# Four down projections of a two-layer block: six of eleven row pairs by seven products in place of eight

## The chip, the cores and the metric

The kernel runs on one core of one Trainium2 chip. Its time is the device time of one execution in microseconds (us); lower is better. The engines are TensorE (PE; its weight loads are listed as PEld), VectorE (DVE), ScalarE (ACT), GpSimd (POOL) and SyncE (SP, which here issues nearly all DMAs).

## The reference, cut to what matters

The program is two layers of a block (feed-forward, mixer, feed-forward, gated embedding), followed by a third block with three attention branches and an MLP, on 256 tokens of width 1024. The change touches the four feed-forwards alone. Each is

```python
def swiglu(x, w_gu, w_down):
    g, u = jnp.split(x @ w_gu, 2, axis=-1)
    return (jax.nn.silu(g) * u) @ w_down

h = h + 0.5 * swiglu(rmsnorm(h, ffn1_norm[i]), ffn1_w_gu[i], ffn1_w_down[i])
```

with `w_gu` of 1024 x 5632 and `w_down` of 2816 x 1024. The product with `w_down` is the down projection: 256 tokens (two blocks of 128) by 22 chunks of 128 rows of `w_down` by 1024 columns (two halves of 512). All of it is float32.

## The kernel before, in words

**A float32 product as three.** TensorE multiplies in a format of fewer bits (`F32R`), so each operand is split into a high part, the value rounded, and a low part, the rest. A product is high x high + high x low + low x high: three matmuls, all added up in one bank of PSUM. The activation (stationary, 128 x 128) and the weights (moving, 128 x 512) are split alike.

**The stream of weight tiles.** `plan_of` lists every weight tile of the program in the order of use, up to 128 x 2048 numbers (1 MB) each. For tile n, SP loads it into one of four slots of `raw` (`load`), ACT copies it to one of three slots of `whi` (high part, ACT's `ahead`, recorded at L1412), DVE subtracts to one of three slots of `wlo` (low part, DVE's `ahead`, L1967), and PE multiplies with both (L564). `take(label)` in an engine's program means: bring this engine's share up to two tiles beyond that label, and for PE wait for that tile. A copy of tile n waits until PE has released tile n - 3. Each engine works strictly through its own list.

**A feed-forward** (`ffn` in each engine's program). For each of 11 chunks c of 256 columns, PE does the up product (two tiles, 48 matmuls), ACT applies Silu (`ftmp`), DVE multiplies by the other half (`fa`), PE transposes `fa` with four transposes (L567, `turn_a`) into bank 4 or 5, and ACT and DVE split the result into `aThi` and `aTlo` (`high_a`, `low_a`). Then comes the down projection (`down`): for column half 0, six weight tiles, token blocks 0 and 1 into banks 6 and 7; then for half 1 six tiles into banks 2 and 3. The last two tiles of a half are taken together, token block 0 first (`closing_block`). In all 44 pairs of chunk and half, 2 token blocks, 3 matmuls: 264 matmuls of 512 columns. Each half is added to the residual `h` by DVE (`residual`, L1970). The transposes of `h` for the next norm (`turn(r, t, 0)`) and what is computed from them (`early_quarters`: `hThi`, `hTlo`) lie in the second half's tiles.

**Where.** The plan is `plan_of` at L156, PE's program `tensor` with `down` at L724 and `ffn` at L743, ACT's `down` at L1466 and `ffn` at L1488, DVE's `down` at L2021 and `ffn` at L2051, POOL's at L2558. The relative-bias table of the attention layer is loaded by SP in `table` (L517), during the up products of the third feed-forward. A small `rstds` on POOL computes the norms' roots.

Of the kernel before, what the change touches and what calls it, by code (L numbers as in the profile page):

```python
# [18 lines left out]
TILE = 2048  # L19

# [23 lines left out]
def constants():  # L44
# [30 lines left out]
    "a_weigh": "exps", "v_outputs": "yev yg yTlo", "a_outputs": "yThi ysq",  # L75
# [69 lines left out]
class Plan:  # L145


    def __init__(self):
        self.tiles, self.index = [], {}

    def add(self, label, pieces, a, b):
        self.index[label] = len(self.tiles)
        self.tiles.append((pieces, a, b))


def plan_of(dr):  # L156
    p = Plan()

    def ffn(i, up, down, extra=None):
        for c in range(11):  # L160
            if extra is not None and c in (0, 2):
                p.add(("pproj", extra, c // 2), [wsrc(dr["ple_w_proj"][extra], 0, 2, c * 256, 512)], 2, 512)
            for k in range(2):
                p.add(("up", i, c, k), [wsrc(up, 4 * k, 4, x * 2816 + c * 256, 256) for x in range(2)], 4, 512)
        for c in range(2):
            for y in range(6):
                nk = min(4, 22 - 4 * y)
                p.add(("down", i, c, y), [wsrc(down, 4 * y, nk, c * 512, 512)], nk, 512)
# [55 lines left out]
PREP = (8, 16, 24)  # L224
HALVES = 2 * len(PREP) + 2
# [129 lines left out]
def programs(dr, mem, banks, plan, ev):  # L355
# [11 lines left out]
    pool_tiles = set()  # L367

    def wview(name, n):
        _, a, b = plan.tiles[n]  # L370
        slots = NRAW if name == "raw" else NSPL
        return mem[name][:, n % slots, 0:a * b].rearrange("p (a b) -> p a b", a=a)

    def wflat(name, n, slots):
        _, a, b = plan.tiles[n]
        return mem[name][:, n % slots, 0:a * b]
# [117 lines left out]
    def sync(S):  # L494
# [3 lines left out]
        def load(n):  # L498
            pieces, a, b = plan.tiles[n]
            slot = wflat("raw", n, NRAW).rearrange("p (a b) -> p a b", a=a)  # L500
            if n >= NRAW:
                last = (n - NRAW,) if n - NRAW > 1 else (n - NRAW, 3)
                S.wait_ge(*at("w_hi", *last))
                S.wait_ge(*at("w_lo" if n - NRAW not in pool_tiles else "w_lo_p", *last))
            c = 0
            for src in pieces:
                wd = src.shape[2]
                e.dma_start(slot[:, :, c:c + wd], src).then_inc(*sig(f"d_w{n % NRAW}", n, by=16))
                c += wd
# [7 lines left out]
        def table():  # L517
            rp = dr["rpb"]
            S.wait_ge(*at("h", 4, 1, 1))
            for y in range(2):  # L520
                src = bass.AP(rp.tensor, 464 - 249 - 15 - (4 - y) * 31, [[1, 64], [465, 16], [1, 250]])
                e.dma_start(mem["tb"][64 * y:64 * y + 64, :, 0:250], src).then_inc(*sig("d_tb", y, by=16))
# [20 lines left out]
        for n in range(2, len(plan.tiles)):  # L543
            if n == tile["yout", 7] + 5:
                pos(0)
            if n == tile["up", 2, 0, 0] + 8:
                table()
            if n == tile["down", 2, 0, 0]:
                pos(1)
            load(n)  # L550
# [9 lines left out]
    def tensor(T):  # L560
# [13 lines left out]
        def take(*label):  # L574
            n = T.n
            T.n += 1
            if tile[label] != n:
                raise ValueError(label)
            T.wait_ge(*at("w_hi", n))
            T.wait_ge(*at("w_lo_p" if n in pool_tiles else "w_lo", n))  # L580
            return wview("whi", n), wview("wlo", n)
# [114 lines left out]
        def closing_block(labels, bs, xhi, xlo, first, between=None):  # L696

            held, k0 = [], first
            for label in labels:
                hi, lo = take(*label)  # L700
                held.append((label, hi, lo, k0))
                k0 += hi.shape[1]
            for t in range(2):
                for i, (label, hi, lo, kk) in enumerate(held):
                    nk = hi.shape[1]
                    for k in range(nk):
                        xh, xl = (y[:, kk + k, t * P:(t + 1) * P] for y in (xhi, xlo))
                        mm(banks[bs[t]], xh, hi[:, k, :], kk + k == 0, False)
                        mm(banks[bs[t]], xh, lo[:, k, :], False, False)
                        last = mm(banks[bs[t]], xl, hi[:, k, :], False, kk + k + 1 == k0)  # L710
                        if between and t and i == 0 and k == 1:
                            between()
                    if t:
                        last.then_inc(*sig(*named(label)))
                    elif i == len(held) - 1:
                        last.then_inc(*sig(*half(label, 0)))
# [7 lines left out]
        def down(name, xhi, xlo, tiles, r, turn_last):  # L724

            for c in range(2):
                bs = ACC[c]
                clear(*bs)
                for y in range(tiles - 2):
# [3 lines left out]
                    if y == 0:  # L733
                        if c == 0:
                            turn_last()
                        elif r < 10:
                            turn(r, 0, 0)
                            turn(r, 1, 0)
                closing_block([name + (c, tiles - 2), name + (c, tiles - 1)], bs, xhi, xlo, 4 * (tiles - 2),
                              (lambda: turn(1, 0, 1)) if c and r == 1 else None)  # L740
                residual_in(r, c, bs)

        def ffn(i, r, extra=None):  # L743
# [24 lines left out]
            down(("down", i), aThi, aTlo, 6, r + 1, lambda: turn_a(10))  # L768
# [636 lines left out]
    def scalar(A):  # L1405
# [8 lines left out]
        def ahead(m):  # L1414
            while A.ready < min(m, len(plan.tiles)):
                n = A.ready
                A.ready += 1
                A.wait_ge(*at(f"d_w{n % NRAW}", n))
                if n >= NSPL:
                    A.wait_ge(*at(*named(plan_labels[n - NSPL])))  # L1420
                copy(wflat("whi", n, NSPL), wflat("raw", n, NRAW)).then_inc(*sig("w_hi", n))
# [44 lines left out]
        def down(name, tiles, r):  # L1466
            for c in range(2):
                for y in range(tiles):
                    if r == 1 and c and y == tiles - 1:
                        square(1, 0, 1)  # L1470
                        high(1, 0, 1)
                    take(*name, c, y)
                    if c and y == 1:
                        if r != 10:
                            early_quarters(r)
                        early_squares(r)
                    if c == 0 and y == 0:
                        yield
            if r == 10:
                square(r, 0, 1)  # L1480
                square(r, 1, 1)
            elif r == 1:
                square(1, 1, 1)
                high(1, 1, 1)
            else:
                late_quarters(r)

        def ffn(i, r, extra=None):  # L1488
            fa, aThi = mem["fa"], mem["aThi"]

            def high_a(c):
                A.wait_ge(*at("turn_a", i, c))
                copy(flat(aThi[:, 2 * c:2 * c + 2, :]), banks[4 + c % 2]).then_inc(*sig("aThi", i, c))
# [17 lines left out]
            for _ in down(("down", i), 6, r + 1):  # L1511
                high_a(10)
# [406 lines left out]
        plan_labels = list(plan.index)  # L1919
# [43 lines left out]
    def vector(V):  # L1963
# [7 lines left out]

        def ahead(m):
            while V.ready < min(m, len(plan.tiles)):
                n = V.ready
                V.ready += 1
                if n in pool_tiles:
                    continue
                V.wait_ge(*at("w_hi", n))
                tt(wflat("wlo", n, NSPL), wflat("raw", n, NRAW), f(wflat("whi", n, NSPL)), ALU.subtract).then_inc(*sig("w_lo", n))
# [41 lines left out]
        def down(name, tiles, r, scalars):  # L2021

            for c in range(2):
                for y in range(tiles):
# [7 lines left out]
                    if c and y == 1 and r != 10:  # L2032
                        early_quarters(r)
            for t in range(2):
                residual(r, t, 1, half(name + (1, tiles - 1), t), ACC[1][t], scalars[t])
                if r == 10:
                    mean_square(10, t)
                if r == 1 and t == 0:
                    low(1, 0, 1)
                    mean_square(1, 0)  # L2040
            if r == 1:
                scaled(0)
            take(*name, 1, tiles - 1)
            if r == 1:
                mean_square(1, 1)
                low(1, 1, 1)
                scaled(1)
            elif r != 10:
                late_quarters(r)

        def ffn(i, r, extra=None):  # L2051
            fa, aThi, aTlo = mem["fa"], mem["aThi"], mem["aTlo"]

            def low_a(c):
                V.wait_ge(*at("aThi", i, c))
                tt(flat(aTlo[:, 2 * c:2 * c + 2, :]), banks[4 + c % 2], f(flat(aThi[:, 2 * c:2 * c + 2, :])), ALU.subtract).then_inc(*sig("aTlo", i, c))
# [16 lines left out]
            for _ in down(("down", i), 6, r + 1, (0.5, 0.5)):  # L2073
                low_a(10)
# [485 lines left out]
    def gpsimd(G):  # L2560
# [5 lines left out]
        def ahead(m):  # L2566
            while G.ready < min(m, len(plan.tiles)):
                n = G.ready
                G.ready += 1
                if n in pool_tiles:  # L2570
                    G.wait_ge(*at("w_hi", n))
                    tt(wflat("wlo", n, NSPL), wflat("raw", n, NRAW), f(wflat("whi", n, NSPL)), ALU.subtract).then_inc(*sig("w_lo_p", n))

        def take(*label):
            ahead(tile[label] + NSPL)

# [59 lines left out]
        def three():  # L2636
            for what, n in three_steps():
                if what == "gate" and n % 2 == 0:
                    take("gate", n // 2)
                elif what == "keep" and n in (3, 7):  # L2640
# [4 lines left out]

        rstds(0)
        rstds(1)
        ssd()
        rstds(2)
        ple_rstd(0)  # L2650
        for r in (3, 4, 5):
            rstds(r)
        natt()
        rstds(6)
        ple_rstd(1)
# [9 lines left out]
def layout(nc):  # L2665
# [29 lines left out]
    def phase(*items):  # L2695
# [3 lines left out]
        if o > 229368:  # L2699
# [4 lines left out]
          ("sg", [P, 2, D]), ("xn", [P, 2, D]), ("pT", [P, 2, 256]), ("pThi", [P, 2, 256], F32R), ("pTlo", [P, 2, 256], F32R))  # L2704
    put("rThi", [P, 8, 256], F32R, z + 48 * 1024)
# [107 lines left out]
```

## Time and profile before

| what | value |
|---|---|
| median of 3 runs | 1677.99 us (1677.39 to 1678.73) |
| profiled execution, first to last instruction (span) | 1676.1 us |
| median less span (what lies around it) | 1.9 us |
| PE busy | 1664.8 us, 99% |
| DVE busy | 1068.0 us, 64% |
| ACT busy | 898.6 us, 54% |
| POOL busy | 86.1 us, 5% |
| mean granted TensorE clock | 0.998 |

The profiled execution's own device time is not listed separately; its span is, and the median of the runs stands 1.9 us above it. Busy time is the time in which an engine had an instruction at work; matmuls overlap in the pipeline, so a busy PE says that it was never out of work, and not how fast it went. Where rows say "idle before <- X", the engine waited that long and X ended the wait. In the rows of the timeline, an instruction that follows its predecessor without a wait starts about 0.08 us before the predecessor's listed end.

### The profile page before, as it was taken

The page shows a single profiled execution, that of the slowest core. Times are in us where ns is not written, and L with a number is a line of the kernel's source. Part 1 is how long each engine was busy: PE and PEld are TensorE (multiplying, and loading weights), DVE is VectorE, ACT ScalarE, POOL GpSimd, SP SyncE. Part 2 cuts the span into 40 slices and gives each one's busy share as a digit, 9 for nine tenths or more (in the row PEclk, how much of TensorE's full clock was granted, in tenths as well). Part 3 has the DMA queues.
Part 4 walks back from the last instruction along what each step waited for, and adds up shares of the span by engine and source line. Part 5 has one row for each costly group of instructions (what it writes and reads, how often), then busy time and mean ns, then how long its engine had stood idle before and what let it go on. Part 6 is the DMA issues. An engine that isn't in the chain of part 4 may idle for free.

```text
span 1676.1 us, 23021 instructions
## 1 busy us (share of the span) xinstructions
PE 1664.8 (99%) x9366; PEld 1426.7 (85%) x9366; DVE 1068.0 (64%) x1364; ACT 898.6 (54%) x1279; POOL 86.1 (5%) x79
## 2 busy tenths in 40 slices
PE   8999999999999999999999999999999999999998
PEld 6888899999788888888888778888889999988886
DVE  5554678999965545755457766555655577766643
ACT  5443566777864444744346665444553556564532
POOL 0000000000100000000007500000000000000000
PEclk9999999999999999999999999999999999999999
DMA  9655567666466554686555336655565533465551
GB/s 306 192 178 184 158 191 208 179 196 209 156 200 198 187 188 165 188 242 209 181 175 195 119 101 214 185 180 188 180 197 153 174 103 126 152 211 178 176 192 60
DMA packets 243978, 300.58 MB, mean 179 GB/s; under 512 B 9248, under 2 KB 175520, under 8 KB 243872
## 3 DMA queue, kind: packets, MB, share of 16 engines
q1 hardware_dynamic: 238224, 289.25, 54.5%
q10 hardware_dynamic: 5648, 9.85, 2.2%
q8 instruction: 75, 1.23, 0.3%
q14 instruction: 31, 0.25, 0.0%
HBM read 297.96 MB, written 1.11 MB: 178 GB/s over the span
## 4 chain that ended last, share of the span: by engine, by line
PE 99%; DVE 1%; DMA 0%; ACT 0%; ACTq 0%; DVEq 0%; issue 0%
PE bank L564 95%; PE bank L567 4%; DMA h<-in_x 0%; DVE wlo L1967 0%; DVE hTlo L1970 0%; DVE xn L1970 0%; DVE h L1970 0%; ACT hThi L1412 0%; DVE xn L2019 0%; DVEq L2740 0%; ACT xn L1409 0%; ACTq L1924 0%; ACTq L1923 0%; ACT L1920 0%; ACTq L2740 0%
## 5 line engine op out<-in xcount | busy, mean ns | idle before, releaser
L1967 DVE TENSOR_TENSOR wlo<-raw,whi 128x2048 fp32r<-128x2048 f32 (+2 forms) x284 | 622.4, 2195 | 326.5 <-ACT whi L1412 326.5
L1412 ACT ACTIVATE whi<-raw 128x2048 fp32r<-128x2048 f32 (+2 forms) x284 | 518.2, 1832 | 244.8 <-PE bank L564 240.9
L564 PE MATMUL bank<-whi,hThi 128*128 128x512 f32 x1056 | 420.7, 398 | 0.0
L564 PE MATMUL bank<-wlo,hThi 128*128 128x512 f32 x1056 | 412.3, 390 | 0.3 <-DVE wlo L1967 0.3
L564 PE MATMUL bank<-whi,hTlo 128*128 128x512 f32 x1056 | 396.8, 391 | 0.0
L564 PE MATMUL bank<-hThi,whi 128*128 128x256 f32 x888 | 253.3, 285 | 0.0
L564 PE MATMUL bank<-hThi,wlo 128*128 128x256 f32 x888 | 251.2, 283 | 0.0
L564 PE MATMUL bank<-hTlo,whi 128*128 128x256 f32 x888 | 251.2, 283 | 0.0
L564 PEld LDWEIGHTS bank<-whi,hThi 128*128 128x128 f32 x1056 | 198.6, 188 | 44.3 <-issue 6.0
L564 PEld LDWEIGHTS bank<-whi,hTlo 128*128 128x128 f32 x1056 | 198.5, 188 | 42.6 <-DVE hTlo L1970 0.3
L564 PEld LDWEIGHTS bank<-wlo,hThi 128*128 128x128 f32 x1056 | 198.8, 188 | 40.5 <-DVE wlo L1967 1.8
L564 PEld LDWEIGHTS bank<-hThi,whi 128*128 128x128 f32 x888 | 169.5, 191 | 3.6 <-issue 3.1
L564 PEld LDWEIGHTS bank<-hThi,wlo 128*128 128x128 f32 x888 | 169.5, 191 | 0.2
L564 PEld LDWEIGHTS bank<-hTlo,whi 128*128 128x128 f32 x888 | 169.5, 191 | 0.2
L564 PE MATMUL bank<-whi,aThi 128*128 128x512 f32 x352 | 137.8, 391 | 0.0
L564 PE MATMUL bank<-whi,aTlo 128*128 128x512 f32 x352 | 137.1, 389 | 0.0
L564 PE MATMUL bank<-wlo,aThi 128*128 128x512 f32 x352 | 137.0, 389 | 0.0
L1412 ACT ACTIVATE aThi<-bank 128x512 fp32r<-128x512 f32 x44 | 26.3, 598 | 155.1 <-PE bank L567 155.1
L1409 ACT ACTIVATE ftmp<-bank,st 128x256 f32<-128x256 f32 x88 | 41.5, 475 | 105.6 <-PE bank L564 105.5
L2564 POOL TENSOR_TENSOR st<-st,cst 128x1 f32<-128x1 f32 (+2 forms) x35 | 36.5, 1057 | 1147.4 <-DVE st L1992 1075.2
L1967 DVE TENSOR_TENSOR aTlo<-bank,aThi 128x512 fp32r<-128x512 f32 x44 | 30.4, 691 | 80.8 <-ACT aThi L1412 80.8
L564 PEld LDWEIGHTS bank<-whi,aTlo 128*128 128x128 f32 x352 | 66.1, 188 | 13.8
(222 smaller groups left out, 1883.4 us busy)
## 6 DMA issues: line engine op xcount, KB each, us to landing
raw<-in_ffn_w_gu SPq DMA_DIRECT2D x172, 512.0 KB, 4.9
raw<-in_ffn_w_down SPq DMA_DIRECT2D x40, 1024.0 KB, 5.0
raw<-in_w_in SPq DMA_DIRECT2D x30, 1024.0 KB, 5.2
raw<-in_ssd_w_in SPq DMA_DIRECT2D x16, 1024.0 KB, 5.6
raw<-in_ssd_w_in SPq DMA_DIRECT2D x32, 512.0 KB, 5.5
raw<-in_w_up SPq DMA_DIRECT2D x16, 1024.0 KB, 5.4
raw<-in_w_down SPq DMA_DIRECT2D x16, 1024.0 KB, 5.0
raw<-in_na_w_qkv SPq DMA_DIRECT2D x12, 1024.0 KB, 5.2
```

The source lines that it names most:

```text
L564: return T.e.matmul(out, lhsT, rhs, start=start, stop=stop, skip_group_check=skip)
L567: return T.e.transpose(out, in_, ident)
L1409: return e.activation(out, in_, func, **kw)
L1412: return e.activation(out, in_, ACT.Identity, **kw)
L1967: return e.tensor_tensor(out, a, b, op)
L2564: return e.tensor_tensor(out, a, b, op)
```

## The change

For six pairs of chunks (2j, 2j + 1), j = 0 to 5, the 2 x 2 x 2 block product (two token blocks, two chunks, two column halves) is computed with seven block products in place of eight, by the scheme of Winograd: a block product is three matmuls as before. The scheme needs four combinations of the weight blocks and four combinations of the activation blocks, and its result in four PSUM banks more (0, 1, 4, 5) that are combined at the end.

- **Plan.** The 1 MB tile `paired` of pair j holds all four weight blocks. It is followed by a tile `mixed` that has no load: its 128 x 2048 numbers are the four combinations, computed by DVE (`sums`) from `raw` into a buffer `ts0` to `ts2`: one instruction of 1024 columns and two of 512, each waiting for the one before. Of `paired` only 1536 columns are split, of `mixed` all 2048. PE uses `paired` for three block products (9 matmuls) and `mixed` for four (12).
- **Order.** The other ten chunks (12 to 21) stay classic, in six tiles of 2 or 4 chunks: `down 0 0`, pair 0, `down 1 0`, pairs 1 and 2, `down 0 1`, pairs 3 to 5, `down 0 2`, and at the end `down 1 1` with `down 1 2`. The transposes of `h` now lie in the last of these.
- **Activations.** During the up products of chunks 1 to 6, ACT copies the transposed bank to `araw`, POOL computes the combinations (`differences`: three subtractions), and ACT and DVE split them (`high_d`, `low_d`).
- **Merging.** After the last pair, ACT copies bank 0 at half scale, DVE does six operations of 512 columns (`merged`), and POOL two additions. Then the residual of the classic products follows.
- **Elsewhere.** The bias table's load moves from the third feed-forward's up products to the start of the attention layer; the row and the transposed embedding of `pos(1)` are loaded there too. An unused branch for tiles split on POOL goes.

```diff
+        rest(0, 0)
+        for j in range(PAIRS):
+            p.add(("paired", i, j), [wsrc(down, 2 * j, 2, 512, 512), wsrc(down, 2 * j, 2, 0, 512)], 2, 1024)
+            p.add(("mixed", i, j), None, 4, 512)
+            if j == 0:
+                rest(1, 0)
+            if j == 2:
+                rest(0, 1)
+        rest(0, 2)
+        rest(1, 1)
+        rest(1, 2)
...
+REST = {(0, 0): (12, 4), (0, 1): (16, 2), (0, 2): (18, 4), (1, 0): (12, 4), (1, 1): (16, 4), (1, 2): (20, 2)}
...
@@ sync: load, table
+                if labels[m][0] == "paired":
+                    S.wait_ge(*at("tsum", *labels[m][1:]))
...
-            S.wait_ge(*at("h", 4, 1, 1))
+            S.wait_ge(*at("w_rel", "mixed", 2, PAIRS - 1))
...
-            if n == tile["up", 2, 0, 0] + 8:
+            if n == tile["qkv", NA_CHUNKS[1], 0]:
                 table()
-            if n == tile["down", 2, 0, 0]:
                 pos(1)
...
@@ tensor: mixed_down
+            def seven(j):
+                first, final = j == 0, j == PAIRS - 1
+                hi, lo = take("paired", i, j)
+                T.wait_ge(*at("aTlo", i, j))
+                T.wait_ge(*at("dTlo", i, j))
+                three_products(0, block_of(2 * j, 0), hi[:, 0, 512:1024], lo[:, 0, 512:1024], first, final)
+                three_products(2, difference(j, 2), hi[:, 1, 0:512], lo[:, 1, 0:512], first, False)
+                three_products(6, block_of(2 * j + 1, 0), hi[:, 1, 512:1024], lo[:, 1, 512:1024], False, False).then_inc(
+                    *sig("w_rel", "paired", i, j))
+                hi, lo = take("mixed", i, j)
+                if first:
+                    clear(4)
+                three_products(4, difference(j, 0), hi[:, 0, :], lo[:, 0, :], first, final)
+                three_products(5, block_of(2 * j, 1), hi[:, 1, :], lo[:, 1, :], first, final)
+                three_products(1, difference(j, 1), hi[:, 2, :], lo[:, 2, :], first, final)
+                three_products(7, block_of(2 * j + 1, 1), hi[:, 3, :], lo[:, 3, :], False, False).then_inc(*sig("w_rel", "mixed", i, j))
...
+            for t in range(2):
+                for k, (hi, lo, y) in enumerate(held):
+                    last = three_products(2 + t, block_of(k0 + k, t), hi, lo, False, k == len(held) - 1)
+                    if t == 0 and k == 2:
+                        turn(r, 0, 0)
+                    if t == 0 and k == 3:
+                        turn(r, 1, 0)
...
@@ scalar: ahead waits for landed(n); for a mixed tile that is "tsum"
+                copy(mem["araw"][:, c % 2, :], b).then_inc(*sig("araw", i, c))
+                copy(aThi[:, 2 * c, 0:P], b[:, 0:P])
+                copy(aThi[:, 2 * c + 1, :], b[:, 256:512]).then_inc(*sig("aThi", i, c))
...
+            def high_d(c):
+                A.wait_ge(*at("dsum", i, c))
+                d = mem["dsum"][:, c % 2, :]
+                copy(aThi[:, 2 * c, P:256], d[:, 0:P])
+                copy(flat(mem["dThi"][:, c, :, :]), d[:, P:512]).then_inc(*sig("dThi", i, c))
...
@@ vector
+        def sums(n):
+            i, j = labels[n][1:]
+            w, o = mem["raw"][:, plan.raw_of[n] % NRAW, :], mem[f"ts{j % 3}"][:, :]
...
+            tt(halves(o[:, 0:1024]), halves(w[:, 512:1536]), w[:, 0:512].unsqueeze(1).to_broadcast([P, 2, 512]), ALU.add).then_inc(*sig("tfirst", i, j))
+            V.wait_ge(*at("tfirst", i, j))
+            tt(o[:, 1024:1536], o[:, 0:512], w[:, 1024:1536], ALU.add).then_inc(*sig("tsecond", i, j))
+            V.wait_ge(*at("tsecond", i, j))
+            tt(o[:, 1536:2048], o[:, 1024:1536], w[:, 1536:2048], ALU.add).then_inc(*sig("tsum", i, j))
...
         def ahead(m):
             while V.ready < min(m, len(plan.tiles)):
                 n = V.ready
                 V.ready += 1
-                if n in pool_tiles:
-                    continue
+                if labels[n][0] == "paired":
+                    sums(n)
                 V.wait_ge(*at("w_hi", n))
...
+            def merged():
+                um, wm = flat(mem["ftmp"][:, :, :]), flat(fa[:, :, :])
+                V.wait_ge(*at("root", i))
+                stt(h[:, 0, chunk(0)], banks[0], 0.5, h[:, 0, chunk(0)], ALU.mult, ALU.add).then_inc(*sig("h11", i))
+                V.wait_ge(*at("w_rel", "mixed", i, PAIRS - 1))
+                stt(um, banks[1], 0.5, um, ALU.mult, ALU.subtract).then_inc(*sig("um", i))
+                stt(h[:, 0, chunk(1)], banks[4], 0.5, h[:, 0, chunk(1)], ALU.mult, ALU.add).then_inc(*sig("h12p", i))
...
+            def mixed_down(r):
+                take("down", i, 0, 0)
+                low_a(10)
+                for j in range(PAIRS):
+                    take("paired", i, j)
+                    take("mixed", i, j)
...
+                merged()
+                take("down", i, 0, 2)
+                V.wait_ge(*at("h21", i))
+                for t in range(2):
+                    residual(r, t, 0, half(("down", i, 0, 2), t), 6 + t, 0.5)
...
@@ gpsimd
+            tt(pairs(d[:, 0:256]), a[:, P:256].unsqueeze(1).to_broadcast([P, 2, P]), outer, ALU.subtract).then_inc(*sig("dpair", i, c))
+            G.wait_ge(*at("dpair", i, c))
+            tt(d[:, 256:384], a[:, 384:512], d[:, 0:P], ALU.subtract).then_inc(*sig("droot", i, c))
+            G.wait_ge(*at("droot", i, c))
+            tt(d[:, 384:512], a[:, 256:384], d[:, 256:384], ALU.subtract).then_inc(*sig("dsum", i, c))
```

## Rows read from the trace of the kernel before

**Rows 1.** The page: its span and the engines' busy time.

```profile
span 1676.1 us, 23021 instructions
PE 1664.8 (99%) x9366; PEld 1426.7 (85%) x9366; DVE 1068.0 (64%) x1364; ACT 898.6 (54%) x1279; POOL 86.1 (5%) x79
```

**Rows 2.** The page: the chain that ended last, by engine.

```profile
PE 99%; DVE 1%; DMA 0%; ACT 0%; ACTq 0%; DVEq 0%; issue 0%
```

**Rows 3.** Chain in order of time, 128 to 215 us: start, length, what.

```profile
131.61 10.93 PE bank L564 x48
142.98 29.96 PE bank L564 x132
173.81 21.78 PE bank L564 x96
195.59 0.44 PE bank L567 x4
196.03 2.77 PE bank L564 x12
```

**Rows 4.** Timeline of ACT, 128 to 210 us: start, length, what, idle before.

```profile
143.01 0.60 ACT L1412 ACTIVATE aThi<-bank 128x512 fp32r<-128x512 f32 x1 [3.60 <-PE bank L567]
143.51 1.91 ACT L1412 ACTIVATE whi<-raw 128x2048 fp32r<-128x2048 f32 x1
```

**Rows 5.** The same of DVE.

```profile
143.65 0.69 DVE L1967 TENSOR_TENSOR aTlo<-bank,aThi 128x512 fp32r<-128x512 f32 x1 [1.90 <-ACT aThi L1412]
145.45 2.29 DVE L1967 TENSOR_TENSOR wlo<-raw,whi 128x2048 fp32r<-128x2048 f32 x1 [1.11 <-ACT whi L1412]
155.08 1.23 DVE L1967 TENSOR_TENSOR wlo<-raw,whi 128x1024 fp32r<-128x1024 f32 x1 [2.29 <-ACT whi L1412]
168.18 2.29 DVE L1967 TENSOR_TENSOR wlo<-raw,whi 128x2048 fp32r<-128x2048 f32 x1 [4.51 <-ACT whi L1412]
170.39 1.28 DVE L1970 SCALAR_TENSOR_TENSOR h<-bank,h 128x512 f32<-128x512 f32 x2
199.43 0.88 DVE L2019 TENSOR_SCALAR xn<-h,st 128x512 f32<-128x512 f32 x2
```

**Rows 6.** Timeline of DVE, 600 to 690 us: an add that waits for DVE itself.

```profile
679.75 0.74 DVE L1970 SCALAR_TENSOR_TENSOR sg<-sg,st,pp 128x512 f32<-128x512 f32 x1
680.53 0.69 DVE L1967 TENSOR_TENSOR h<-h,sg 128x512 f32<-128x512 f32 x1
```

**Rows 7.** Chain in order of time, whole run: the second and the last down projection.

```profile
610.64 29.96 PE bank L564 x132
1133.40 29.97 PE bank L564 x132
```

**Rows 8.** Groups by form: busy us, mean ns, idle before.

```profile
L2564 POOL TENSOR_TENSOR gate<-gate 128x512 f32<-128x512 f32 x6 | 9.7, 1616 | 248.8 <-DVE EW L1967 244.9 <-ACT gate L1409 4.0
```

**Rows 9.** Stretches: busy us (count) of PE, PEld, DVE, ACT, POOL, PEclk, DMA, GB/s.

```profile
20.00:130.00 110.00, 110.00 (x503) 90.82 (x502) 62.84 (x52) 53.88 (x58) 1.06 (x2) 1.00 0.66 211
4.00:8.00 4.00, 1.48 (x7) 0.67 (x5) 0.00 (x0) 0.78 (x4) 0.00 (x0) 1.00 0.97 316
8.00:10.00 2.00, 1.76 (x6) 1.21 (x6) 1.61 (x5) 1.48 (x6) 0.00 (x0) 0.51 1.06 373
```

**Rows 10.** Timeline of the opening, two matmuls of 512 columns.

```profile
10.76 0.63 PE L564 MATMUL bank<-whi,hThi 128*128 128x512 f32 x1
11.19 0.51 PE L564 MATMUL bank<-whi,hTlo 128*128 128x512 f32 x1
```

**Rows 11.** Timelines of POOL and of DVE from 895 us: both at work.

```profile
895.95 7.29 POOL L2564 TENSOR_TENSOR bm<-tb,cst 128x256 f32<-128x256 f32 x8
...
896.68 2.75 DVE L1967 TENSOR_TENSOR wlo<-raw,whi 128x2048 fp32r<-128x2048 f32 x1
```

**Rows 12.** DMA issues: count, KB each, us to landing.

```profile
raw<-in_ffn_w_down SPq DMA_DIRECT2D x40, 1024.0 KB, 5.0
tb<-in_rpb SPq DMA_DIRECT2D x2, 1000.0 KB, 14.6
```


## What was predicted

> **What bounds the kernel now.** I read the page's busy times first. The reader is to see PE at work for 1664.8 of 1676.1 us while DVE has 64% [rows 1]; then the chain that ended last, which gives PE 99% [rows 2]. So a matmul less is worth its spacing, as long as no other engine takes the end of that stage. The chain in order of time shows the first down projection as unbroken blocks of matmuls [rows 3]: 132 in 29.96 us, 0.227 us each. The second and the last look the same, 29.96 and 29.97 us [rows 7], so one walk serves all four. Last I read DVE and ACT in that stretch [rows 4, 5]: they sleep between tiles and wait for PE to release a slot. That slack is what the change spends.
>
> **What is removed.** A pair goes from 24 matmuls to 21, so a projection loses 18 and the program 72. At 0.227 us that is 4.09 us per projection, 16.3 us in all, if nothing is late.
>
> **What is added on DVE.** Prices: 128x2048 takes 2.29 us alone and 2.21 us to the next one's start; 1024 columns 1.23 [rows 5]; 512 columns 0.69, between plain float32 tiles in SBUF too, with a start 0.04 us after the end of what it waits for on its own engine (679.75 + 0.74 to 680.53) [rows 6]. By these slopes 1536 columns are 1.76. ACT takes 1.91 for 2048 and starts its next some 0.1 before the end [rows 4]; DVE starts 0.02 to 0.04 after ACT's end. One pair on DVE:
> - sums: 1.23 + 0.04 + 0.69 + 0.04 + 0.69 = 2.69 us;
> - the low part of `paired` starts 0.08 before that end and takes 1.76: over at 4.37;
> - meanwhile ACT can copy `mixed` only from 2.69 + 0.03, for 1.92: done at 4.64;
> - the low part of `mixed` starts at 4.68 and gives DVE free 2.21 later: 6.89 us.
>
> PE needs 21 x 0.227 = 4.77 us for the pair. Before, the same 1 MB of weights cost DVE 2.21 against 5.45 on PE. So inside the pairs DVE is the bound by 2.1 us a pair. The classic tiles between give back 5.45 - 2.21 = 3.2 (one of 4 chunks), 2.72 - 1.14 = 1.6 (one of 2).
>
> **The walk through one projection**, on the clock of the first. Up to the transposes of chunk 10 nothing changes for PE: sums of pair 0 and its low part run from 132.9 to 137.3 in the stretch where DVE waited before; the last `fa` is out near 138.1, and PE transposes it only at 142.5. `aTlo` of chunk 10 comes at 143.65, and the next low part (now `down 1 0`) at 145.45, as before [rows 5]. From there DVE has no idle time but what is inside a pair:
> - `down 1 0`: 145.45 + 2.21 = 147.66;
> - pairs 1 to 5: 5 x 6.89 = 34.45, and `down 0 1`: 1.14. Together 183.25;
> - `down 0 2` and `down 1 1`: 4.42. 187.67;
> - `merged`, six of 512 columns, 0.61 apart as the two residuals of 1.28 show [rows 5], with a wait or two inside: 3.66. 191.33;
> - `down 1 2`: 1.22, and 0.04 to PE: 192.59.
>
> PE on the same clock: pair 0 from 142.95, `down 1 0` 147.77 to 153.21, pair 1 to 157.98. It would start pair 2 there but gets its low part at 158.9: the first stall. From then it waits some 0.6 us before each `mixed` and, after `down 0 1`, 1.6 before each of pairs 4 and 5. `down 0 2` runs from 186.1 to 191.5, and then PE waits to 192.59, because it takes `down 1 1` and `down 1 2` at once. 36 matmuls (8.17) and two groups of transposes (0.88) follow: 201.64. Before, the same point, without the third group of transposes (0.44), was 196.03 + 2.77 - 0.44 = 198.36 [rows 3]. So a projection becomes 3.28 us **longer**: 4.1 won in matmuls, 7.4 lost in stalls.
>
> What is queued behind DVE's waits: in a pair, the `mixed` low part waits for ACT's copy with the next pair's sums behind it, for which PE waits. In `merged` DVE waits for ACT's copy of bank 0 (from 184.7) and the last matmul of pair 5 (186.1), both past at 187.7, so these cost nothing. POOL's two additions (1.62 each [rows 8]) end near 193, before DVE asks for them at 198.4.
>
> **Transposes and next stage.** `h` of half 0 is ready at 193.2 and 193.8, PE turns it at 194.6 and 195.8, and the split is over at 198.5; the next stage begins after 201.6. Cost nothing; if DVE came 3 us later still, PE would also wait at the turn. In the first projection alone the transposes of `h` 0, half 1 come six matmuls into block 1, at 198.9, and its residual, held behind that split, is out at 199.1: 0.2 us more.
>
> **The up products.** DVE has 62.84 busy of 110 us there, ACT 53.88, POOL 1.06 [rows 9]; a chunk is 11.37 us (10.93 + 0.44), so ACT works 5.6 of it. It gains four copies of at most 512 columns (under 0.60 each [rows 4]), DVE 0.8 us or so, POOL three subtractions of under 1.62 [rows 8]. From the transposes (131.6) by 0.60 + 3 x 1.62 the combination is there at 137.1, and ACT asks for it after `ftmp` at 137.6. Its weight copies come up to 0.8 us later, with PE over 5 us behind. Cost nothing; should POOL be twice as slow, ACT's next copy would come 4 us later and still in time.
>
> **DMA.** Bytes are the same; 1 MB in 6.9 us is slower than before, and a load lands 5.0 us after issue [rows 12] while four slots give over 10 us. The table (2 loads, 14.6 us to landing [rows 12]), `pos(1)` and two weight tiles now go out together near the third projection's end. POOL took the table at 895.95 [rows 11], about 16 us into the attention stage; it would land before. I cost it at 0, its bounds being 0 and 5 us (a tile that comes one landing late).
>
> **Sum.** 4 x 3.28 + 0.2 = 13.3 us. The span goes from 1676.1 to 1689.4; the median stood 1.9 above the span, so 1678.0 + 13.3 = 1691.3 us.
>
> **Unknown prices, both ends.** The trace shows no sum of float32 tiles with a repeated operand. From below: one-source operations on SBUF took 0.44 us per 512 columns (the last of [rows 5]); at that rate the three sums save 1.02 us a pair, 5 x 1.02 = 5.1 a projection, -1.8 in place of +3.3: 1671. From above: with POOL at work 2048 columns took 2.75 for 2.29 [rows 11], a factor 1.20; on the sums +0.52 a pair, 2.6 a projection: 1702. I take 0.69, because the addition `h<-h,sg` is the same kind of instruction on the same memory [rows 6], and POOL is idle during the pairs. The Trainium skill, "VectorE: DVE Perf Modes", section "Mode 2×_2P — use both read ports for one tensor", says that float32 operations of one source can go at twice the rate while a two-source one can't, its second port being busy. These rows agree (0.44 against 0.69), which speaks against the lower end.
>
> **The rivals.**
> - Only the matmuls count. DVE hides all of it: -16.3 us, 1661.7. For it: DVE idles half of the stretch now. Against: 6.89 against 4.77 in a pair, and at most three tiles of `wlo` to run ahead on. 3%.
> - The other side: cheap sums. The mechanism sits in `sums`; it decides from 3.28 / 5 = 0.66 us less per pair, so below 6.23 us the kernel is faster, down to 1671. 4%. Around that point, within 0.2%, lie 4%.
> - Dear sums or dear waits: a pair of 7.4 us, 1698 to 1702. 9%.
> - The clock. In the opening PE worked 1.48 of 4 us, and then the granted clock was 0.51, the level of 1.2 GHz, with 0.43 us between matmuls [rows 9, 10]. If the gaps (PE at work 69% of a pair) did this from pair 1 to `down 0 2`, 141 matmuls would take 60.6 us where the walk has 39.4: 21 us more a projection, 1776. Against: every other stretch was at 1.00, and no gap here passes 1.6 us. 4%. The Trainium skill's "TensorE: Matmul & The Clock Gate", section "A second HAM failure mode: psum-queue depth-cycling", describes frequent small idle times that make the clock swing; no row of this trace shows it in mid-kernel.
>
> **How the numbers follow.** DVE as the bound, at the prices read: 76%, 1685 to 1698 (a pair of 6.6 to 7.2 us, and the table). The range for 8 in 10 reaches up into dear sums: 1684 to 1702. About 0.2%, 3.4 us, is what a measurement can tell from no change. Slower: 76 + 9 + 4, 89%; same 4%; faster 3 + 4, 7%.
>
> **What would show it.** 72 matmuls of 512 columns fewer; PE at 97 to 98% busy with idle time released by DVE `wlo`, some 7 us in each projection and none elsewhere; DVE in a pair 6.9 us from sum to sum with ACT's copy of `mixed` on its path; the chain running through DVE between pair 2 and `down 1 2`. Wrong it is if the sums of 512 columns last well under 0.69, if PE shows no gaps, if the clock falls, or if gaps appear in the up products or at the start of the attention stage.

## The result

| kernel | median, us | fastest to slowest | ratio to before, 95% interval |
|---|---|---|---|
| before | 1678.36 | 1677.39 to 1679.18 | |
| changed | 1700.28 | 1698.92 to 1701.60 | 1.013 [1.0116, 1.0144] |

The change makes the kernel slower by 21.9 us; forecast were 13.3, with a range of 1684 to 1702. The page of the changed kernel, its span, the engines' busy time and the chain by engine (against [rows 1, 2]):

```profile
span 1696.7 us, 23401 instructions
PE 1659.9 (98%) x9294; PEld 1411.4 (83%) x9294; DVE 1203.5 (71%) x1556; ACT 959.6 (57%) x1403; POOL 138.6 (8%) x159
...
PE 86%; DVE 8%; ACT 3%; issue 2%; DMA 0%; ACTq 0%; DVEq 0%
```

72 matmuls went. The span grew all the same, and 14% of the chain runs through other engines, where it was 1%.

**Where the time went.** From PE's timeline I took, for each of the four projections, the time from its first matmul's start to 0.227 us after its last one's start, and the stretches between. All in us:

| | projection 1 | 2 | 3 | 4 | between 1, 2 | between 2, 3 | between 3, 4 | after 4, to the last matmul's start |
|---|---|---|---|---|---|---|---|---|
| before | 61.69 | 61.21 | 61.25 | 61.26 | 405.97 | 149.59 | 250.71 | 480.13 |
| changed | 66.91 | 67.52 | 65.93 | 65.93 | 405.96 | 149.63 | 250.70 | 480.15 |

Everything outside the projections is the same within 0.04 us. The projections cost 5.22, 6.31, 4.68 and 4.67 more, 20.9 together, and the spans differ by 20.6 (the opening took 0.3 less). The medians differ by 21.9: the profiled execution of the changed kernel, 1698.92 us, is the fastest of its four, and where the others take their 0.5 to 2.7 us more no trace shows. Three parts are to be told apart: 4.67 in each, 0.54 more in the first, 1.6 more in the second.

DVE in the first projection (start, length, what, idle before; it answers to [rows 5]):

```profile
145.12 2.29 DVE L2109 TENSOR_TENSOR wlo<-raw,whi 128x2048 fp32r<-128x2048 f32 x1 [1.11 <-ACT whi L1524]
147.33 1.22 DVE L2109 TENSOR_TENSOR ts<-raw 128x1024 f32<-128x1024 f32 x1
148.59 1.42 DVE L2109 TENSOR_TENSOR ts<-ts,raw 128x512 f32<-128x512 f32 x2
149.92 1.75 DVE L2109 TENSOR_TENSOR wlo<-raw,whi 128x1536 fp32r<-128x1536 f32 x1
152.00 2.29 DVE L2109 TENSOR_TENSOR wlo<-ts,whi 128x2048 fp32r<-128x2048 f32 x1 [0.32 <-ACT whi L1524]
154.20 1.22 DVE L2109 TENSOR_TENSOR ts<-raw 128x1024 f32<-128x1024 f32 x1
...
182.77 4.49 DVE L2109 TENSOR_TENSOR wlo<-raw,whi 128x2048 fp32r<-128x2048 f32 x2
187.18 0.69 DVE L2112 SCALAR_TENSOR_TENSOR h<-bank,h 128x512 f32<-128x512 f32 x1
...
190.17 0.82 DVE L2109 TENSOR_TENSOR h<-h,fa 128x512 f32<-128x512 f32 x1
190.91 2.29 DVE L2109 TENSOR_TENSOR wlo<-raw,whi 128x1024 fp32r<-128x1024 f32 x1
193.13 1.27 DVE L2112 SCALAR_TENSOR_TENSOR h<-bank,h 128x512 f32<-128x512 f32 x2
```

Read it against the walk: `down 1 0`, then sums of 1024 and twice 512 columns, the low part of `paired`, 0.3 us of idle time for ACT, the low part of `mixed`, and from 147.33 to 154.20 one pair is over: 6.87 us, forecast 6.89. The merging starts at 187.18 (forecast 187.67, on a run that is 0.3 us earlier throughout). Then the row at 190.91: 1024 columns in 2.29 us, where [rows 5] have 1.23. ACT in the same place, the copy of `mixed` starting as the sums end:

```profile
143.18 3.28 ACT L1524 ACTIVATE whi<-raw 128x2048 fp32r<-128x2048 f32 x2
150.04 1.92 ACT L1524 ACTIVATE whi<-ts 128x2048 fp32r<-128x2048 f32 x1 [3.57 <-DVE ts L2109]
```

POOL, in the stretch of the merging:

```profile
189.14 1.30 POOL L2770 TENSOR_TENSOR h<-h,ftmp 128x512 f32<-128x512 f32 x1 [100.76 <-DVE h L2112]
190.40 1.72 POOL L2770 TENSOR_TENSOR h<-h,fa 128x512 f32<-128x512 f32 x1
```

DVE's operation starts at 190.91 in the trace, POOL's second addition ended at 190.40 + 1.72 = 192.12, and DVE was done 1.08 us after that, which is what the work on 1024 columns takes (1.07, by 2.29 for 2048 and 1.22 for 1024). The same 2.29 us stand there in all four projections. DVE's last merging operation, two SBUF sources as well, took 0.82 for 0.69, while POOL's first was ending. The merging operations with a PSUM source stayed at 0.68. PE before the closing tiles and at the late transposes:

```profile
191.04 0.39 PE L604 MATMUL bank<-whi,aTlo 128*128 128x512 f32 x1
193.35 0.47 PE L604 MATMUL bank<-whi,aThi 128*128 128x512 f32 x1 [1.92 <-DVE wlo L2109]
193.66 0.40 PE L604 MATMUL bank<-wlo,aThi 128*128 128x512 f32 x1
...
199.60 0.39 PE L604 MATMUL bank<-whi,aTlo 128*128 128x512 f32 x1
200.30 0.63 PE L607 MATMUL bank<-cst,h 128*128 128x128 f32 x4 [0.32 <-DVE h L2112]
```

PE waits 1.92 us for that low part; later 0.32 us for the residual of half 1. Last, stretches of the changed kernel (busy us of PE, PEld, DVE, ACT and POOL with counts, then PEclk, DMA share, GB/s), the first answering to [rows 9]:

```profile
20.00:130.00 110.00, 110.00 (x503) 91.00 (x502) 67.50 (x70) 59.30 (x82) 11.23 (x20) 1.00 0.65 210
620.00:655.00 35.00, 30.89 (x130) 23.57 (x129) 33.09 (x27) 17.98 (x11) 0.00 (x0) 1.00 0.52 167
...
663.90:666.20 2.30, 0.39 (x2) 0.01 (x1) 2.30 (x2) 1.81 (x1) 1.09 (x1) 1.00 0.56 213
667.00:669.00 2.00, 2.00 (x6) 1.54 (x5) 2.00 (x2) 0.00 (x0) 0.00 (x0) 0.50 0.67 214
670.00:672.00 2.00, 2.00 (x14) 1.74 (x13) 0.23 (x1) 1.41 (x6) 0.00 (x0) 0.93 0.92 284
```

The up products (first row) still have PE at work for all 110 us, with DVE at 67.50, ACT at 59.30 and POOL at 11.23. In the second projection's pairs DVE is busy 33.09 of 35 us. And behind the gap of that projection the granted clock fell to 0.50, the level of 1.2 GHz, for some 3 us: the nine matmuls up to the first transposes took 3.4 us in place of 2.2, and the four transposes 0.68 in place of 0.35, from start to start.

### The profile page after: what moved, and what is told of

The parts are those of the page before. It is cut to its first block, busy times and chain, and to the rows that moved or that the text cites. A ratio compares the mean times of both kernels' runs of the same rounds, so it can differ in the third digit from the quotient of the medians.

```text
span 1696.7 us, 23401 instructions
## 1 busy us (share of the span) xinstructions
PE 1659.9 (98%) x9294; PEld 1411.4 (83%) x9294; DVE 1203.5 (71%) x1556; ACT 959.6 (57%) x1403; POOL 138.6 (8%) x159
## 4 chain that ended last, share of the span: by engine, by line
PE 86%; DVE 8%; ACT 3%; issue 2%; DMA 0%; ACTq 0%; DVEq 0%
PE bank L604 83%; PE bank L607 4%; DVE wlo L2109 3%; DVE ts L2109 3%; ACT whi L1524 3%; DVE h L2112 0%; DMA h<-in_x 0%; DVE h L2109 0%; DVE fa L2112 0%; DVE ftmp L2112 0%; DVE rTlo L2112 0%; DVE hTlo L2112 0%; DVE xn L2112 0%; ACT rThi L1524 0%; ACT hThi L1524 0%
## 5 line engine op out<-in xcount | busy, mean ns | idle before, releaser
L2109 DVE TENSOR_TENSOR wlo<-raw,whi 128x2048 fp32r<-128x2048 f32 (+3 forms) x284 | 613.0, 2163 | 211.6 <-ACT whi L1524 211.6
L1524 ACT ACTIVATE whi<-raw 128x2048 fp32r<-128x2048 f32 (+3 forms) x284 | 508.4, 1797 | 157.7 <-PE bank L604 154.1
L604 PE MATMUL bank<-whi,aThi 128*128 128x512 f32 x256 | 103.1, 403 | 20.4 <-issue 12.3
L604 PE MATMUL bank<-whi,aTlo 128*128 128x512 f32 x256 | 100.5, 393 | 0.0
L604 PE MATMUL bank<-wlo,aThi 128*128 128x512 f32 x256 | 100.2, 391 | 0.0
L2109 DVE TENSOR_TENSOR aTlo<-bank,aThi 128x128 fp32r<-128x128 f32 (+2 forms) x68 | 28.8, 453 | 76.5 <-ACT aThi L1524 76.4
L1524 ACT ACTIVATE whi<-ts 128x2048 fp32r<-128x2048 f32 x24 | 46.0, 1915 | 59.0 <-DVE ts L2109 59.0
L604 PEld LDWEIGHTS bank<-whi,aThi 128*128 128x128 f32 x256 | 48.2, 188 | 37.2 <-issue 28.2
```

Of the source, the lines that this page charges most:

```text
L604: return T.e.matmul(out, lhsT, rhs, start=start, stop=stop, skip_group_check=skip)
L1524: return e.activation(out, in_, ACT.Identity, **kw)
L2109: return e.tensor_tensor(out, a, b, op)
```

## The experiments

Each was run on one chip with the kernel before (medians 1677.97 us beside e1 to e4, 1677.94 beside e5 to e7). The changed kernel's 1700.28 was measured beside 1678.36, so differences of a few tenths against it say nothing. e2 and e3 leave out part of the computation, as their expectations say.

**e1, the last tile ahead of the merging.**

```diff
             def mixed_down(r):       # vector
...
-                merged()
                 take("down", i, 0, 2)
+                merged()
```

> DVE makes the low part of the tile down 1 2 before the six merging operations; nothing else moves. Theory (DVE's strict order ahead of the closing tiles is what is late, and POOL's additions hold up that one operation by 1.07 us): the operation takes 1.23 us, PE finds the tile ready, the gap of 1.92 us before the closing tiles goes in all four projections, and with it the fall of the clock seen in the second. About 2.2 us a projection less than the changed kernel, plus 1.6 once: near 1690 us (1688 to 1692). Rival (the tail is bound by the merging and the transposes of h, whatever the order): PE then waits at the transposes for h instead, and the time stays within 2 us of 1700.

Measured: 1689.20 us, ratio 1.0066 [1.0051, 1.0081], 11.1 less than the changed kernel. The projections took 64.74, 63.74, 63.74 and 63.79, 2.2 us less than the changed kernel's, and 3.8 less in the second. DVE:

```profile
183.78 5.63 DVE L2109 TENSOR_TENSOR wlo<-raw,whi 128x2048 fp32r<-128x2048 f32 x3
189.33 0.68 DVE L2112 SCALAR_TENSOR_TENSOR h<-bank,h 128x512 f32<-128x512 f32 x1
...
192.32 0.80 DVE L2109 TENSOR_TENSOR h<-h,fa 128x512 f32<-128x512 f32 x1
193.16 1.29 DVE L2112 SCALAR_TENSOR_TENSOR h<-bank,h 128x512 f32<-128x512 f32 x2
```

Three low parts stand together: 5.63 us, so the last takes 1.2. No gap is left before the closing tiles, and no projection shows matmuls at the lower clock's spacing. The last two operations of these rows stand beside POOL's second addition (192.54 to 194.27): those from PSUM still take 0.64 us each. The rival falls: the transposes had slack for it.

**e2, POOL's additions cut to 8 columns.**

```diff
-            tt(h[:, 0, chunk(1)], h[:, 0, chunk(1)], flat(mem["ftmp"][:, :, :]), ALU.add).then_inc(*sig("h12", i))
+            tt(h[:, 0, 512:520], h[:, 0, 512:520], flat(mem["ftmp"][:, :, :])[:, 0:8], ALU.add).then_inc(*sig("h12", i))
...
-            tt(h[:, 1, chunk(1)], h[:, 1, chunk(1)], flat(mem["fa"][:, :, :]), ALU.add).then_inc(*sig("h22", i))
+            tt(h[:, 1, 512:520], h[:, 1, 512:520], flat(mem["fa"][:, :, :])[:, 0:8], ALU.add).then_inc(*sig("h22", i))
```

> Leaves out all but 8 of 512 columns of POOL's two additions to h after the merging; all waits stay. Theory (a DVE operation with two SBUF sources stands still while POOL works): the 1024-column operation takes 1.23 us for 2.29, 1.1 to 1.2 us less a projection, 4 to 5 in all, near 1696 us. Rival (the weight loads at 280 to 380 GB/s at that moment slow it): it stays at 2.29 us and the time at 1700.

Measured: 1693.07 us, 7.2 less than the changed kernel; projections 65.70, 64.73, 64.73, 64.72, so 1.2 less each, and in the second the fall of the clock is gone as well. DVE, last merging operation and last low part:

```profile
191.00 0.68 DVE L2109 TENSOR_TENSOR h<-h,fa 128x512 f32<-128x512 f32 x1
191.60 1.22 DVE L2109 TENSOR_TENSOR wlo<-raw,whi 128x1024 fp32r<-128x1024 f32 x1
```

0.68 and 1.22 us for 0.82 and 2.29. The DMA queues moved 347 GB/s during that low part, and 285 during the slow one of the changed kernel, so the rival (the weight loads) falls. The size in my expectation was short by the 1.6 us of the clock; together with the 1.2 each that makes 6.4 us in the projections, and the last 0.8 of the 7.2 I didn't trace. POOL's two operations of 8 columns:

```profile
189.97 0.20 POOL L2770 TENSOR_TENSOR h<-h,ftmp 128x8 f32<-128x8 f32 x1 [100.75 <-DVE h L2112]
191.23 0.51 POOL L2770 TENSOR_TENSOR h<-h,fa 128x8 f32<-128x8 f32 x1 [1.06 <-DVE h L2112]
```

It works the other way round too. The first stands beside operations of DVE that read PSUM and takes 0.20 us; the second starts inside DVE's last merging operation (191.00 + 0.68 = 191.68) and ends 0.06 us after it.

**e3, no sums.**

```diff
             if labels[n][0] == "mixed":
-                return mem[f"ts{labels[n][2] % 3}"][:, :]
+                return mem["raw"][:, plan.raw_of[n - 1] % NRAW, :]
...
-            tt(o[:, 1024:1536], o[:, 0:512], w[:, 1024:1536], ALU.add).then_inc(*sig("tsecond", i, j))
+            tt(o[:, 1024:1088], o[:, 0:64], w[:, 1024:1088], ALU.add).then_inc(*sig("tsecond", i, j))
```

(the first and the third sum likewise, all cut to 64 columns a block; SP waits for the `mixed` splits before it loads over `raw`)

> Leaves out the sums of the weights: three operations of 64 columns a pair are left and the mixed tile is split from the loaded blocks as they are. Theory (DVE's 6.9 us a pair is the bound): a pair costs DVE some 4.7 us, under PE's 4.77, the stalls inside the pairs go, and only the one before the closing tiles is left (2.3 us with POOL's additions). Walked with the same durations: 1.6 us a projection less than the kernel before, 1672 us (1669 to 1675). Rival (only the matmuls count, 18 less at 0.227): 1662. Rival (something other than the sums, the extra copies and combinations of the up products among it, costs the time): above 1680.

Measured: 1679.06 us (1675.82 to 1681.24), ratio 1.0005 [0.9996, 1.0015]. That is 21 less than the changed kernel, but 7 above my number and 4 above the top of my range, and 1 short of where the second rival began. DVE in one pair, and the last low part:

```profile
168.27 0.28 DVE L2111 TENSOR_TENSOR ts<-raw 128x128 f32<-128x128 f32 x1
168.59 0.48 DVE L2111 TENSOR_TENSOR ts<-ts,raw 128x64 f32<-128x64 f32 x2
168.99 1.75 DVE L2111 TENSOR_TENSOR wlo<-raw,whi 128x1536 fp32r<-128x1536 f32 x1
171.06 2.29 DVE L2111 TENSOR_TENSOR wlo<-raw,whi 128x2048 fp32r<-128x2048 f32 x1 [0.32 <-ACT whi L1526]
173.27 0.28 DVE L2111 TENSOR_TENSOR ts<-raw 128x128 f32<-128x128 f32 x1
...
186.69 2.28 DVE L2111 TENSOR_TENSOR wlo<-raw,whi 128x1024 fp32r<-128x1024 f32 x1
```

A pair now takes DVE 5.0 us at most, and PE shows no gap inside the pairs above 0.39 us from start to start. The projections took 61.50, 60.48, 62.32 and 60.54: the second and the fourth are 0.7 below before, walked were 1.6. What the walk lacked is seen on PE: each time it resumes matmuls of 512 columns behind a wait or a transpose, the first spacing is 0.31 for 0.227 us, seven times in the second projection (before: twice); PE waits 0.27 for the low part of `down 1 0`; and two first `mixed` matmuls of a pair come 0.1 late. The third projection had the fall of the clock again. So a gap of 2.61 us before the closing tiles stays with next to nothing left of the sums, which the rival "only the matmuls count" has no place for. Nor does the second rival explain the time: the copies and combinations of the up products still run here, and the stretches between the projections are as before within 0.04 us.

**e4, four pairs, last tile ahead.**

```diff
-PAIRS = 6
+PAIRS = 4
-REST = {(0, 0): (12, 4), (0, 1): (16, 2), (0, 2): (18, 4), (1, 0): (12, 4), (1, 1): (16, 4), (1, 2): (20, 2)}
+REST = {(0, 0): (8, 4), (0, 1): (12, 4), (0, 3): (16, 2), (0, 2): (18, 4),
+        (1, 0): (8, 4), (1, 3): (12, 4), (1, 1): (16, 4), (1, 2): (20, 2)}
+ORDER = (0, (1, 0), 1, (0, 1), 2, (1, 3), 3, (0, 3))
```

(numbers are pairs, brackets classic tiles; every engine's loop follows `ORDER`; and e1's edit)

> Four pairs in place of six, 14 chunks classic, one classic tile behind each pair, and the low part of the last tile ahead of the merging. Theory: pair and classic tile cost DVE 6.9 + 2.2 = 9.1 us and PE 4.8 + 5.4 = 10.2, so PE never waits; 12 matmuls of 0.227 us less a projection, 2.7 us, 10.9 in all: 1667.5 us, faster than before. Rival (each pair has a cost outside DVE's sums, such as the banks, the transposes or the merging): no faster than 1675.

Measured: 1669.29 us, ratio 0.9948 [0.9933, 0.9963]: **faster than both kernels**, 8.7 us or 0.5% under the one before. The longest piece of the chain in the second projection, then DVE over one pair and its classic tile:

```profile
613.54 41.09 PE bank L604 x180
```

```profile
623.50 1.22 DVE L2107 TENSOR_TENSOR ts<-raw 128x1024 f32<-128x1024 f32 x1
624.75 1.42 DVE L2107 TENSOR_TENSOR ts<-ts,raw 128x512 f32<-128x512 f32 x2
626.09 1.75 DVE L2107 TENSOR_TENSOR wlo<-raw,whi 128x1536 fp32r<-128x1536 f32 x1
628.16 2.29 DVE L2107 TENSOR_TENSOR wlo<-ts,whi 128x2048 fp32r<-128x2048 f32 x1 [0.32 <-ACT whi L1523]
631.50 2.29 DVE L2107 TENSOR_TENSOR wlo<-raw,whi 128x2048 fp32r<-128x2048 f32 x1 [1.05 <-ACT whi L1523]
633.71 1.22 DVE L2107 TENSOR_TENSOR ts<-raw 128x1024 f32<-128x1024 f32 x1
```

180 matmuls follow each other without a stop. From sums to sums 10.21 us pass on DVE (623.50 to 633.71), of which 1.4 are idle (0.32 and 1.05). PE needs 10.2 for its 45 matmuls and sets the pace. Projections: 60.01, 58.96, 58.98, 59.01, so 1.7 less than before in the first and 2.3 in the others, walked were 2.7. In the others the 0.4 are two more restarts (0.2) and the wait for `down 1 0` (0.27).

**e5, six pairs, sums one pair ahead** (and e1's edit).

```diff
-                if labels[n][0] == "paired":
+                if labels[n][0] == "paired" and labels[n][2] == 0:
                     sums(n)
+                if labels[n][0] == "mixed" and labels[n][2] + 1 < PAIRS:
+                    sums(tile["paired", labels[n][1], labels[n][2] + 1])
```

> Six pairs, the last tile ahead of the merging, and on DVE the sums of pair j+1 moved in front of the low part of mixed j. Theory (DVE's own time before the closing tiles is what counts, not where in it an operation lies): the 0.31 us a pair in which DVE waited for ACT's copy is filled and the first sums start in DVE's idle time before 143 us; the closing tiles come 2.9 us earlier than with the last tile moved alone, which makes 1676 to 1678 us, level with before. Each mixed tile comes later behind its paired tile, so PE's gaps move from in front of paired to in front of mixed. Rival (each gap before mixed is added to PE's time): 1689 us or more.

Measured: 1679.35 us, ratio 1.0009 [0.9999, 1.0018], 9.8 less than e1 and 1.4 above the top of my range. Projections 62.30, 61.33, 61.38, 61.37. PE's two gaps, both in front of `mixed` (`dThi` is the high part of the combined activations):

```profile
628.35 0.39 PE L604 MATMUL bank<-whi,aTlo 128*128 128x512 f32 x1
630.25 0.47 PE L604 MATMUL bank<-whi,dThi 128*128 128x512 f32 x1 [1.51 <-DVE wlo L2109]
...
642.50 0.39 PE L604 MATMUL bank<-whi,aTlo 128*128 128x512 f32 x1
644.30 0.47 PE L604 MATMUL bank<-whi,dThi 128*128 128x512 f32 x1 [1.42 <-DVE wlo L2109]
```

1.90 and 1.80 us from start to start. Ten microseconds from the order of DVE's list alone; what stalls are left cost as much as 72 matmuls bring. The rival (1689 or more) falls.

**e6, five pairs, sums ahead** (classic tiles (1, 0), (0, 1), (1, 3) between; e1's and e5's edits).

```diff
+PAIRS = 5
+ORDER = (0, (1, 0), 1, (0, 1), 2, (1, 3), 3, 4)
```

> Five pairs, three classic tiles between them, last tile and sums ahead. Theory: 15 matmuls less a projection (3.4 us) and about 1.1 us of stalls: 2.2 us less a projection than before, 1669 us (1667 to 1671), the same as four pairs. Rival (only DVE's total against PE's total counts, and five pairs fit): 1665.

Measured: 1672.08 us, ratio 0.9966 [0.9953, 0.9979]; projections 60.53, 59.53, 59.70, 59.61. It is 3 us over my number and 1 over the top of my range: the restarts, which that sum lacked too, and one gap of 1.22. Against e4, the fifth pair takes away three matmuls (0.68 us) and its projections are 0.5 to 0.7 longer all the same, so it costs 1.2 to 1.4 in stalls.

**e7, four pairs, last tile behind the merging** (e4 without e1's edit).

```diff
             def mixed_down(r):       # e4 with
...
-                take("down", i, 0, 2)
                 merged()
+                take("down", i, 0, 2)
```

> Four pairs, but the last tile's low part behind the merging as in the changed kernel. Theory: no stall at the pairs, but the one before the closing tiles (2.3 us) is back, whatever the number of pairs, because the merging waits for the last pair and POOL's additions hold up the operation behind it: 1678 to 1680 us, no gain over before. Rival (the gap before the closing tiles is only DVE's backlog from the pairs): with no backlog it is under 0.5 us and the time is 1669 us, that of four pairs with the tile ahead.

Measured: 1683.99 us (1682.30 to 1687.37), ratio 1.0038 [1.0023, 1.0053], 14.7 over e4, and 4 over the top of my range. Projections 62.50, 63.08, 63.00, 61.49. DVE and then PE in the second:

```profile
650.10 2.29 DVE L2107 TENSOR_TENSOR wlo<-raw,whi 128x2048 fp32r<-128x2048 f32 x1 [0.43 <-ACT whi L1523]
...
656.03 2.28 DVE L2107 TENSOR_TENSOR wlo<-raw,whi 128x1024 fp32r<-128x1024 f32 x1
```

```profile
655.82 0.39 PE L604 MATMUL bank<-whi,aTlo 128*128 128x512 f32 x1
658.46 0.47 PE L604 MATMUL bank<-whi,aThi 128*128 128x512 f32 x1 [2.25 <-DVE wlo L2107]
...
659.56 0.63 PE L604 MATMUL bank<-wlo,aThi 128*128 128x512 f32 x1
659.99 0.63 PE L604 MATMUL bank<-whi,aTlo 128*128 128x512 f32 x1
```

The gap is 2.64 us from start to start though DVE had been idle until 650.10, one low part before the merging; so the rival (only backlog) falls. Then the spacing is 0.43, the clock at 0.50. It fell in the second and third projection, 1.6 and 1.5 us, which my sum did not have. One more 0.5 us is in the stretch between 3 and 4, with POOL's bias operations on the chain; no other run shows it, and I left it open.

## Why the prediction was right or wrong, by its own steps

- **The number: partly luck.** 1700.28 lies above 1685 to 1698, where the forecast put 76%, and in the stretch to which it gave 9% for dear sums or dear waits, a pair of 7.4 us. Neither came: a pair took 6.87 us. The range reached far enough for a reason that did not happen, and was filled by two others, POOL's hold on DVE and the clock.
- **Direction and mechanism: right.** The step "inside the pairs DVE is the bound" is shown by its rows (6.87 us a pair), by e3, which takes nearly all of the sums away and gets 21 us back, and by e4, where a pair and a tile fit under PE and the gaps vanish.
- **The removal, 18 matmuls of 0.227 us a projection: right.** Between gaps, spacing and count are as forecast.
- **Term too small: 3.28 us a projection, measured 4.67.** The step that failed is "POOL's two additions (1.62 each) end near 193, before DVE asks for them at 198.4", which I had at no cost. I asked who waits for their result, and not what they hold up while they run: 1.07 us on the last low part and 0.13 on the last merging operation. e2 gives back 1.2 a projection. With it the sum is 4.48; the remaining 0.2 fits the slower first spacings after the gap and at the split transposes, which no run separates. I had a row that hints at it, DVE's 2.75 us beside POOL [rows 11], and used it as a factor on the sums, where POOL is idle. The Trainium skill's "GPSIMD Engine Reference", section "Specifications", has it that POOL shares its SBUF interface with VectorE, with contention for DVE operations in a two-port mode or with two SBUF sources. The runs here agree for two SBUF sources: such an operation took 2.29 us for 1.22 beside POOL, those with a PSUM source stayed at 0.68. No run here shows the two-port mode.
- **First projection, 0.2 forecast, 0.54 measured.** The residual of half 1 was as late as said, plus the lateness of the whole tail (the wait of 0.32 at 200.30, and a fourth restart).
- **The clock: given as a rival at 21 us a projection, came as 1.6 us once.** Wrong was its place and size. In the pairs, where PE stood for at most 1.6 us at a time (1.9 in e5), it never fell. It fell only behind the pause before the closing tiles, 2.28 to 2.64 us from start to start: in 4 of the 12 projections profiled that have this pause (changed kernel 1, e3 1, e7 2), and in none of the 20 without (in e2 it is 1.1 us, in e1, e4, e5 and e6 there is none before the closing tiles). It came back within 3 to 3.6 us each time. Why it fell in these four and not in the other eight, behind the same pause, stays open.
- **No cost in the up products and the table: right.** The stretches between the projections are unchanged. The transposes of half 0 had no wait in front of them either, not even in e1, where the closing tiles come 2.2 us earlier.
- **"Cheap sums", "only the matmuls": fell.** 512 columns took 0.69, and even without sums the merging leaves a gap.

What I did not forecast is that the gap before the closing tiles has a second cause. I counted the last low part as one more term of DVE's backlog, and in the changed kernel it is: DVE has no idle time between the last pair and that row. e7 shows that the gap is there with that backlog gone. In its second projection ACT may copy `down 1 1` only when PE has released the last pair's tile (648.1). Then follow that copy (1.9 us), its low part (2.2), the merging (3.7) and the low part of `down 1 2` (2.3), 10.2 us together, and PE has 36 matmuls to cover them, 8.2 us. The reason in my expectation, that the merging waits for the last pair, is not what the rows show: there is no wait in front of it.

## What to carry to other kernels

Saved matmuls are worth their spacing only while the engine that feeds them has time left in that very stretch: work out the helper's microseconds per unit against PE's and choose how many units to convert by that balance (here four gave 1669 us, five 1672 and six, at best, 1679). Put what PE will want next ahead of bookkeeping that nobody awaits yet; that alone was 11 us, 1.6 of them the clock's. Work given to POOL to spare DVE must be laid beside DVE operations that read PSUM, or where DVE is idle.

## What the hardware showed that I had not expected

A DVE operation with two SBUF sources did not slow down beside a POOL addition, it stood until POOL was done: 2.29 us for 1.22, ending 1.08 us after POOL, in all four projections; and POOL's 8 columns stood until such an operation of DVE was done (0.51 us for 0.20). TensorE's clock fell to the lower of its two levels behind one pause of 2.3 to 2.6 us, and in a third of the cases only. That this spreads the executions of one kernel (1675.8 to 1681.2 in e3) is likely and not shown, since one of each kernel is traced: the fastest of e3 has a mean granted clock of 0.998 and the slowest 0.995. A first matmul of 512 columns after a wait or a transpose is followed at 0.31 us and not at 0.227.
